# First attention with fp32r values in high and low columns and normalising on GpSimd: what it does to a kernel that TensorE bounds

## The reference

```
def mla_mixer(hn, positions, w_in, q_norm_g, kv_norm_g, w_uq, w_ukv):
    ...
    kv = (rmsnorm(c_kv, kv_norm_g) @ w_ukv).reshape(b, s, MLA_HEADS, MLA_NOPE + MLA_V)
    k_nope, v = kv[..., :MLA_NOPE], kv[..., MLA_NOPE:]
    ...
    o = causal_dense_attention(q, k, v)        # 12 heads, 96 wide keys, 64 wide values
def one_block(args):                           # 128 queries of one head
    sc = jnp.where(mask[None, None], sc, NEG)
    p = jax.nn.softmax(sc, axis=-1).astype(v.dtype)
    return jnp.einsum('bhqk,bkhd->bqhd', p, v)
def memory_cross_attention(q_cross, mem_n, w_mem_kv):
    kv = (mem_n @ w_mem_kv).reshape(b, N_MEM, 2, MEM_HEADS, HEAD_DIM)
    ...
x = x + jnp.concatenate([mix, cross], axis=-1) @ w_o[i]
```

## Time and profile before

| | |
|---|---|
| median of 3 runs | 1883.83 us (1883.49 to 1885.21) |
| profiled execution | 1883.43 us, span 1881.6 us |
| PE busy | 1863.9 us (99%) |
| PEld busy | 1551.9 us (82%) |
| DVE busy | 876.1 us (47%) |
| ACT busy | 791.6 us (42%) |
| POOL busy | 994.5 us (53%) |
| granted clock of PE | 0.999 in the mean |

### The profile page before, as it was taken

How to read it: one execution, slowest core, us unless ns; L and a number is a source line. 1 busy time by engine, 2 the same in 40 slices (tenths; PEclk the granted TensorE clock), 3 DMA queues, 4 the chain that set the end, 5 groups by cost and what they waited for, 6 DMA issues and landing times.

```text
span 1881.6 us, 26687 instructions
## 1 busy us (share of the span) xinstructions
PE 1863.9 (99%) x9075; PEld 1551.9 (82%) x9075; DVE 876.1 (47%) x1784; ACT 791.6 (42%) x1416; POOL 994.5 (53%) x1300
## 2 busy tenths in 40 slices
PE   9999999999999999999999999999999999999999
PEld 6878888888888888888888888887778888888887
DVE  6877642222236676422222673697752354444200
ACT  6658642323233576432232353646642333233221
POOL 6740265455556642655555564455465456555553
PEclk9999999999999999999999999999999999999999
DMA  6330133323322212332323323221023322332332
GB/s 218 119 105 1 40 101 101 95 96 100 99 91 90 81 44 69 106 99 93 101 90 99 101 79 99 70 78 35 24 90 100 96 92 93 100 100 89 112 101 78
DMA packets 47437, 168.29 MB, mean 89 GB/s; under 512 B 5616, under 2 KB 5872, under 8 KB 47088
## 3 DMA queue, kind: packets, MB, share of 16 engines
q1 hardware_dynamic: 46368, 164.64, 27.3%
q10 hardware_dynamic: 976, 2.39, 0.5%
HBM read 164.13 MB, written 2.10 MB: 88 GB/s over the span
## 4 chain that ended last, share of the span: by engine, by line
PE 91%; DVE 5%; ACT 2%; issue 1%; DMA 0%; POOL 0%; SPq 0%; DVEq 0%; ACTq 0%
PE bank L644 27%; PE bank L645 27%; PE bank L646 27%; PE bank L729 3%; PE bank L775 3%; PE bank L766 2%; PE bank L747 1%; DVE ACC L1450 1%; PE bank L742 0%; ACT WH L1039 0%; DVE KT L1497 0%; DMA X<-x 0%; PE bank L937 0%; DVE KML L1525 0%; PE bank L687 0%
## 5 line engine op out<-in xcount | busy, mean ns | idle before, releaser
L586 POOL TENSOR_TENSOR WL<-RAW,WH 128x256 fp32r<-128x256 f32 x1208 | 938.1, 808 | 809.2 <-ACT WH L1039 808.8
L644 PE MATMUL bank<-XH,WH 128*128 128x512 f32 x1311 | 521.5, 398 | 1.4 <-DVE VM L1741 0.7
L646 PE MATMUL bank<-XH,WL 128*128 128x512 f32 x1311 | 510.8, 390 | 0.0
L645 PE MATMUL bank<-XL,WH 128*128 128x512 f32 x1311 | 510.6, 389 | 0.0
L1039 ACT ACTIVATE WH<-RAW 128x1024 fp32r<-128x1024 f32 x302 | 316.9, 1051 | 301.2 <-PE bank L646 297.6
L646 PEld LDWEIGHTS bank<-XH,WL 128*128 128x128 f32 x1311 | 246.0, 188 | 52.0
L644 PEld LDWEIGHTS bank<-XH,WH 128*128 128x128 f32 x1311 | 246.3, 188 | 50.8 <-DVE VM L1741 1.1
L645 PEld LDWEIGHTS bank<-XL,WH 128*128 128x128 f32 x1311 | 246.5, 188 | 47.4 <-issue 0.7
L644 PE MATMUL bank<-HH,WH 128*128 128x512 f32 x512 | 199.2, 389 | 0.0
L645 PE MATMUL bank<-HL,WH 128*128 128x512 f32 x512 | 199.2, 389 | 0.0
L646 PE MATMUL bank<-HH,WL 128*128 128x512 f32 x512 | 199.2, 389 | 0.0
(11 more groups left out here) (378 smaller groups left out, 2813.1 us busy)
## 6 DMA issues: line engine op xcount, KB each, us to landing
RAW<-stream SPq DMA_DIRECT2D x302, 512.0 KB, 3.5
out<-X SPq DMA_DIRECT2D x8, 256.0 KB, 4.6
X<-x SPq DMA_DIRECT2D x3, 512.0 KB, 7.6
MEM<-mem SPq DMA_DIRECT2D x1, 1024.0 KB, 10.7
W<-cmp_w ACTq DMA_DIRECT2D x1, 1024.0 KB, 4.7
KT<-KR ACTq DMA_DIRECT2D x1, 768.0 KB, 6.6
CT<-consts SPq DMA_DIRECT2D x1, 513.0 KB, 11.6
X<-x SPq DMA_DIRECT2D x2, 256.0 KB, 3.5
```

Of the source, the lines that this page charges most:

```text
L586: ins = pool.tensor_tensor(WL[:, slot, c], RAW[:, slot, c], WH[:, slot, c].bitcast(F32), ALU.subtract)
L644: pe.matmul(dst, lhs[0], rhs[0], start=start, stop=False)
L645: pe.matmul(dst, lhs[0], rhs[1], start=False, stop=False)
L646: return pe.matmul(dst, lhs[1], rhs[0], start=False, stop=stop)
```

## The change

- mla's own heads get the paired form (`paired=True` per unit; `PAIRED` becomes a property of a unit). `VALUE_LAG` of mla goes from 7 to 8. The memory heads keep the form they had.
- The values become fp32r, 64 high columns beside 64 low ones: heads 0 to 5 in `V0`, 6 to 8 in free slots of `XH`, 9 to 11 of `XL` (`v0_block`, `v0_columns`). ACT makes the high part, DVE the low part, and DVE drains the output (`value_low`).
- The high and low transposed rows lie in `XH` and `XL` (`PARTS`).
- POOL normalises all 64 units of mla (`NORMED_BY_POOL`), and makes the low parts of layer 0's memory keys in eight pieces between them, at units 8, 12, ... 36. PE waits for these ahead of the memory heads instead of ahead of the attention.
- The first of a head's value matmuls is high x (unit 3 and small rows), and its low partner goes to the end of the group.
- In nsa, DVE drains the gate with j == 4 two units later, at 51 instead of 49.

```diff
-TURN_LAG, VALUE_LAG = 5, {"mla": 7, "swa": 7, "nsa": 8}
-PAIRED = ("nsa",)
+TURN_LAG, VALUE_LAG = 5, {"mla": 8, "swa": 7, "nsa": 8}
+NORMED_BY_POOL = ("mla", "nsa")
...
-                V0 = tensor(mla, "V0", [P, NT, NH * HD])
+                V0 = tensor(mla, "V0", [P, NT, V0_HEADS, 2 * HD], F32R)
...
-                         [V0[:, kb, blk(h // 2)] for kb in range(b + 1)], h % 2, blk(b),
+                         [v0_block(h, kb) for kb in range(b + 1)], 0, blk(b), paired=True,
...
+            def memory_key_low(piece):
+                j, half, to = piece // 4, piece // 2 % 2, piece % 2
+                at, rows = slice(j * NMEM, (j + 1) * NMEM), slice(HD * half, HD * half + HD)
+                pool.wait_ge(signal("split_hi"), 3 + j)
+                ins = pool.tensor_tensor(KML[HD * to:HD * to + HD, 0, 2 * j + half, :], PT1[rows, 0, at],
+                                         KMH[rows, 0, 2 * j + half, :].bitcast(F32), ALU.subtract)
...
+            def normalise(name, i):
+                units, prob, _ = ATTENTION[name]
+                row, c = prob[i % len(prob)][:, units[i].keys], i % 8
+                pool.wait_ge(signal(name + "_summed"), i + 1)
+                pool.tensor_scalar(row, row, RS[:, c:c + 1], units[i].weight, ALU.mult, ALU.mult
+                                   ).then_inc(signal(name + "_prob"), 1)
+
             lo_parts(0, converted("wo0"))
+            for i in range(len(ATTENTION["mla"][0])):
+                normalise("mla", i)
+                if 8 <= i < 40 and i % 4 == 0:
+                    pool.wait_ge(signal("mla_prob"), i + 1)
+                    memory_key_low(i // 4 - 2)
...
-                        order = [(j, 0), (j - 2, 1), (j, 1), (j, 2), (j, 3)]
-                        for last, kb in reversed(order) if u.stop else order:
-                            for part in (PTH, PTL):
...
+                        order = [(last, kb, part) for last, kb in ((j, 0), (j - 2, 1), (j, 1), (j, 2), (j, 3))
+                                 for part in (high, low)]
+                        if u.start:
+                            order = order[:1] + order[2:] + order[1:2]
...
-            attention("mla", (signal("split_lo"), SPLIT_AT["mem"] + 2))
+            attention("mla", (signal("split_lo"), SPLIT_AT["mem"]), memory=(signal("split_lo"), SPLIT_AT["mem"] + 2))
...
-                act.wait_ge(drained, o)
-                act.activation(V0[:, b, first:first + n], BANK[o % RING][:, 0:n], ACT.Copy, scale=RKV[:, b:b + 1]
-                               ).then_inc(drained, 1)
+                for part, c in v0_columns(b, first, n):
+                    ins = act.activation(part[:, :, 0:HD], BANK[o % RING][:, c].rearrange("p (h n) -> p h n", n=HD), ACT.Copy,
+                                         scale=RKV[:, b:b + 1])
+                ins.then_inc(signal("v0_hi"), 1)
...
+            def value_low(o, b, first, n):
+                bank = output(o)
+                dve.wait_ge(signal("v0_hi"), (b if first == 0 else NT + b) + 1)
+                for part, c in v0_columns(b, first, n):
+                    ins = dve.scalar_tensor_tensor(part[:, :, HD:2 * HD], bank[:, c].rearrange("p (h n) -> p h n", n=HD),
+                                                   RKV[:, b:b + 1], part[:, :, 0:HD].bitcast(F32), ALU.mult, ALU.subtract)
+                ins.then_inc(drained, 1)
+
             scale_columns("c_q", P * KQ, factor=-MLA_SCALE, of_normed=True, dst=RQ)
+            for b in range(NT):
+                value_low(memo + 4 + b, b, 0, 8)
             for j in range(2):
                 split_lo_q(j, PROB1[:, j, :], QX[:, 2 * j:2 * j + 2, :])
-            dve.wait_ge(drained, memo + MEM1)
...
-            for j in range(2):
-                split_lo_k(2 + j, PROB1[:, 2, j * NMEM:(j + 1) * NMEM], KMH[:, 0, 2 * j:2 * j + 2, :],
-                           KML[:, 0, 2 * j:2 * j + 2, :])
...
+                            if u.paired:
+                                own.then(dve.tensor_tensor(HEAD_LOW[0:HD, :], bank[0:HD, :], hi.bitcast(F32), ALU.subtract))
+                                dve.tensor_tensor(lo, bank[HD:P, :], HEAD_LOW[0:HD, :], ALU.add).then_inc(signal(name + "_lo"), 1)
+                            else:
...
-            late |= {max(GATE_AT[KD * j + KD - 1] + 1, 2 * NT * (j + 1)): early_gate(j) for j in range(2 * EARLY_GATES)}
+            late |= {max(GATE_AT[KD * j + KD - 1] + 1 + 2 * (j == 4), 2 * NT * (j + 1)): early_gate(j)
+                     for j in range(2 * EARLY_GATES)}
```

More of the change, by code:

```diff
@@ L488, in program, with values_before @@
         HEAD_LOW = SIN2
+        PARTS = {"mla": [part[:, 0:NT, :].rearrange("p a (c n) -> p (a c) n", c=2) for part in (XH, XL)],
+                 "swa": [None, None], "nsa": [PTH, PTL]}
+        def values_before(name, j):
+            paired = sum(u.paired for u in ATTENTION[name][0])
+            return j // NT if j < paired else paired // NT + j - paired
         def turned_part(part, j):
@@ L626, in _ @@
             lo_parts(early, plan.out_tile[plan.out0["gates"]] + 1)
-            units, prob, _ = ATTENTION["nsa"]
             tile = plan.out_tile[plan.out0["gates"]] + 1
[L629 to L633, removed]
+            for i in range(len(ATTENTION["nsa"][0])):
+                normalise("nsa", i)
                 for j in range(2 * EARLY_GATES):
@@ L702, in scales, with attention @@
                 return step
-            def attention(name, *ready, meanwhile={}):
+            def attention(name, *ready, meanwhile={}, memory=None):
                 units, prob, pt = ATTENTION[name]
+                high, low = PARTS[name]
                 for sem, value in ready:
@@ L732, in attention @@
                     j = i - VALUE_LAG[name]
-                    if 0 <= j and name in PAIRED and j % NT == NT - 1:
+                    if 0 <= j and units[j].paired and j % NT == NT - 1:
                         u = units[j]
@@ L742, in attention @@
                             pe.matmul(bank[0:HD, :], VC[:, at, HD * g:HD * g + HD], PCT[:, g, :], start=False, stop=False)
[L743 to L748 removed]
+                        order = [(last, kb, part) for last, kb in ((j, 0), (j - 2, 1), (j, 1), (j, 2), (j, 3))
+                                 for part in (high, low)]
+                        if u.start:
+                            order = order[:1] + order[2:] + order[1:2]
+                        elif u.stop:
+                            order = order[::-1]
+                        for n_pass, (last, kb, part) in enumerate(order):
+                            turned, to = turned_blocks(part, last, kb, bank)
+                            ins = pe.matmul(to, u.values[kb], turned, start=n_pass == 0 and (u.start or not u.stop),
+                                            stop=n_pass == len(order) - 1 and u.stop)
                         ins.then_inc(signal(name + "_values"), 1)
@@ L768, in attention @@
                     j = i - VALUE_LAG[name]
-                    if 0 <= j and name not in PAIRED:
+                    if 0 <= j and not units[j].paired:
                         u = units[j]
@@ L1111, in attention @@
                                        accum_out=SUM[:, c:c + 1]).then_inc(signal(name + "_exp"), 1)
[L1112 to L1117, removed]
+                    for j in (i - VALUE_LAG[name] - 1, i - VALUE_LAG[name]):
+                        if 0 <= j < n and units[j].head_end and units[j].paired == (j + VALUE_LAG[name] == i):
+                            u = units[j]
+                            act.wait_ge(signal(name + "_values"), values_before(name, j) + 1)
+                            act.activation(u.head_end[0], BANK[HEAD_OUT[name][u.head % 2]][u.out_rows, :], ACT.Copy
+                                           ).then_inc(signal(name + "_hi"), 1)
             def output_projection(stage, norm, x_stage, meanwhile=None):
```

95 lines of the change are left out of this document (60 added, 35 removed).

## The result

The changed kernel takes 1888.16 us (median of 13 runs, 1886.95 to 1889.55) against 1883.83 us: the ratio is 1.0023, 95% interval 1.0015 to 1.0031. That is 4.3 us slower, 1.2 us above the forecast, and the 0.2% at which the prediction parted same from slower lies inside the interval. The profiled execution took 1888.78 us, 5.35 above that of before.

A forecast was written before the change was run, and what follows sets the result against it. PE bounds the kernel now; in the changed own heads a ring of PE, ACT and DVE would. Terms -1.2 - 1.3 + 3.3 + 3.6 - 0.4 - 0.5 = +3.5 us; forecast 1887.0 us, range 1878 to 1893.

The forecast's parts named there:

- the ring: First attention, own heads: a dependent loop over PE, ACT and DVE walked once per head, 5.87 us; 1887 us, chance 0.64.
- the two ways round: Own heads, from DVE's subtraction to the next 512-key exponential: 3.11 us over PE, 3.04 us over DVE and ACT.
- rival B: Own heads: PE stays last, 12 x -0.8 = -9.6 us; total about 1872.5 us, chance 0.11.
- before the attention: DVE loses eight key subtractions and gains the values' low parts; PE's query outputs come sooner: -1.2 us (+1.5 to -2.0).
- from there to the exponential of unit 11: Start of the first attention, from the first reduction: 9.8 us instead of 11.07, -1.3 us.
- nine rounds: Own heads of the first attention: each round 5.87 instead of 5.50 us, 9 x 0.37 = +3.3 us.
- transition: From own heads to memory heads, where the last three own heads end: 19.7 us instead of 16.09, +3.6 us.
- end of the attention: DVE no longer blocks the last normalisation, one more step of lag is paid: -0.4 us (0 to -0.8).
- gate drain: Second block's attention: the drain leaves its place in the ring and goes two units on, -0.5 us (0 to -0.6).
- rival E: Own heads: PE's idle gaps lower its clock, PE's 4.7 us double, 12 heads cost some 40 us; chance 0.02.
- Making one shorter would not help.: Own heads: both ways round close at almost the same length, 3.04 and 3.11 us, so shortening one gains nothing.
- The new wait ahead of layer 1's first memory output: Before the attention: that output waits for an early value's low part, now on DVE: +0.8 us, wait under 1 us.

The follow-up runs named there:

- experiment 4: Three separate edits of the changed kernel's own heads: one low instruction instead of two, 1877.55 us; half the value matmuls, 1885.84 us; both low instructions one unit later, 1889.89 us.
- experiment 3: The changed kernel with the low parts of layer 0's memory keys back on DVE ahead of the attention, none on GpSimd: 1893.21 us, ratio 1.0047.
- experiments 1: The kernel before, with only DVE's drain of the gate with j == 4 made two units later: 1882.36 us, ratio 0.9993.
- experiment 2: The kernel before, with only the normalising of the first attention moved from DVE to GpSimd: 1883.53 us.
- the last version: Changed kernel: low rows copied by ACT, added by GpSimd; head copy and lows one unit later; last two own heads' lows on DVE at once: 1876.65 us.

## Why the prediction was right, and where its terms were off

Its likeliest case, the ring, is what the chain shows, and experiment 4 confirms it by taking one element out: a low instruction gives back more than its own length, half of PE's value matmuls nearly nothing. That the two ways round cross in DVE's order it had not seen; the run with the low instructions moved showed it. Two sums slipped: 1883.83 + 3.5 is 1887.3 and not 1887.0, and rival B's 1872.5 leaves out the start (-1.3). The terms, profile against profile:

| term | forecast | measured |
|---|---|---|
| start of the launch, up to PE's first `MH_` product | 0 | +0.61 |
| from there to the first reduction (before the attention) | -1.2 | -1.67 |
| from there to the exponential of unit 11 | -1.3 | -1.00 |
| nine rounds | +3.3 | +4.19 |
| transition | +3.6 | +5.03 |
| end of the attention | -0.4 | -0.23 |
| up to the second block's attention | 0 | -0.96 |
| gate drain | -0.5 | -0.60 |
| sum | +3.5 | +5.37 |

*The rounds.* Mis-sized: 5.97 for 5.87 us. The one head end of the earlier trace rows had the head copy 0.70 us behind the exponential; here that holds for every second head, and the others have 0.83. The value matmuls took 1.49 and not 1.44. PE's own work, 4.75 us a round, and its 1.2 us of idle time came as forecast. The 4.92 us of its busy column (44.25 us in nine rounds) are not a measure of it: in the run with the lows one unit later PE has the same instructions and 49.29 us in that column.

*The transition.* Mis-sized by 1.4 us, 0.9 to 1.0 of them by the clock. The ring went on to the last own head with waits of 2.05 and 1.53 us, and after the first of these the set of value matmuls took 2.37 us (194.99 to 197.36) in place of 1.49, because the granted clock had fallen. In the run of experiment 3, with the same instructions from there on, that set started at 200.15, before the clock fell, and the transition took 20.17 us (196.51 to 216.68) in place of 21.12. I had given rival E two chances in a hundred, on the ground that 1.81 us of idle time had passed unpunished in the earlier trace rows. It came once, for 0.9 us. The stretches, changed kernel:

```profile
194.00:196.00 2.00, 1.01 (x5) 0.97 (x6) 1.91 (x9) 0.73 (x4) 0.48 (x1) 0.85 0.00 0
196.00:198.00 2.00, 2.00 (x11) 1.82 (x9) 0.94 (x5) 0.66 (x3) 0.95 (x2) 0.50 0.00 0
```

*"Making one shorter would not help."* Right for the way over PE (0.11 us for 0.75). Wrong for the ways' common part: the low instructions stand in both, and there a shortening is worth its full length.

*Before the attention.* Right in direction, and near in size by luck: experiment 3 shows each side to be several us. The +0.61 us ahead of it are of the launch and not of the change. From the first `MH_` product to the first reduction the seven other executions with the same instructions up to there took 66.94 to 67.00 us, and the three of the old form (the kernel before, experiments 1 and 2) 68.66 to 68.68: this part repeats to a few hundredths. Ahead of that product the seven lie between 1.09 us earlier and 0.92 us later than the kernel before. The new wait ahead of layer 1's first memory output did not appear; PE waited 0.35 us ahead of an earlier value output, at 81.09. The low parts of 384 and 128 columns took 0.60 and 0.34 us, a pair 0.79 start to start (forecast 0.75), those of 64 and 192 columns 0.52 (0.5). In experiment 3 five of the memory keys' subtractions of 256 columns took 4.32 us, 0.86 each, with GpSimd busy beside them for all 4 us of that stretch. So a column cost 1.6 ns in the 384-column low part and 3.4 ns in the keys' subtraction: the lower bound was the right one. The kernel before holds a direct comparison, the same subtraction for layer 1's keys, from 213.24 us, where GpSimd's conversions end at 214.71:

```profile
211.70 3.01 POOL L586 TENSOR_TENSOR WL<-RAW,WH 128x256 fp32r<-128x256 f32 x4 [81.06 <-ACT WH L1039]
213.24 4.46 DVE L1525 TENSOR_TENSOR KML<-KMV,KMH 64x256 fp32r<-64x256 f32 x8 [1.98 <-ACT KMH L1066]
215.02 0.42 DVE L1525 TENSOR_TENSOR KML<-KMV,KMH 64x256 fp32r<-64x256 f32 x1
```

The first two, which start beside GpSimd, took 0.87 and 0.85 us, the other six 0.42 each. The Trainium skill (SBUF - State Buffer, Who interferes with whom) says that a DVE instruction with two SBUF inputs contends with a GpSimd instruction that reads SBUF, and that one with at most one SBUF input does not, outside the modes in which DVE uses both of its ports; by that rule the keys' subtractions pay and the values' low parts, which read PSUM and one SBUF tile, don't, and the traces agree.

*Start.* Of the 1.00 us the normalising alone gave 0.24 (experiment 2). The value matmuls that come one unit later and take less time are left for the rest, which is argued and not shown; with half of them the stretch took 9.96 us in place of 10.07.

*Open.* Between the end of the first attention and the second block's attention 0.96 us of the lag disappear. About 0.6 of them lie at one place, in layer 1's attention. The kernel before has a normalisation of 256 columns on DVE there that took 0.90 us (at 644.82, beside a GpSimd conversion) and the changed kernel one of 0.35 us (at 651.63), and PE waits of 0.28 us (645.77) and 0.55 us (647.17) in the one and of 0.19 us (652.55) in the other. The two longer waits show in experiments 1 and 2 as well, and in two versions of the changed kernel (lows one unit later, and head copy later after it); the other six versions have the short one. So it is not the form of the values that decides there. The rest of the 0.96 us stays open. The medians differ by 4.3 us and the two profiled executions by 5.4. Part of this is the clock: 0.6 us at the start of the launch and about 0.9 at 195 us are of these two executions, and the mean granted clock of the changed kernel's runs was 0.997 to 0.999.

## What to carry to other kernels

When a change gives work to engines that stand in a loop with the bound one, walk the loop in program order before pricing busy time: here 0.75 us less PE work a head cost 0.5 us a head, while 20% of PE's time lay idle. Measure such idle time from start to start: a busy column whose ends are modelled hid 0.2 us of it a head here, and all of it in the last version. Then look for a second way round of nearly the same length; moving an instruction within an engine's order helps only if it leaves both, and the slot to look for is one where that engine waits for another anyway. And where the form of the work changes, look at the banks that both forms share: the last units of the one form must be finished early, before the first of the other need their banks, even if that costs the loop something.

## What the runs showed that I had not expected

Short idle stretches can cost the clock. PE waits of 0.98 to 1.13 us in each of nine rounds left the granted clock at 1.00, and so did waits of 2.19 and 2.39 us, one each, in two of the later versions. But it fell to 0.50 after the wait of 2.05 us above, in experiment 3 after that of 3.19 us and again after one of 2.05 us (at 200.15), and in the run with half the value matmuls, where each round had 1.50 or 1.64 us, after the fourth of these (at 158.10), where the second, as long, had left it at 1.00; it fell there twice more by 194 us. The stretches of that run:

```profile
158.00:160.00 2.00, 1.90 (x10) 1.86 (x11) 1.89 (x10) 1.57 (x6) 1.27 (x3) 0.66 0.00 0
160.00:162.00 2.00, 2.00 (x9) 1.71 (x8) 1.64 (x8) 2.00 (x5) 1.40 (x3) 0.50 0.00 0
```

So the length of a single wait did not decide it by itself in these runs. The Trainium skill (TensorE: Matmul & The Clock Gate, What's actually happening) has the clock set by how busy PE was recently, watched at a pace that runs free of the kernel; by that rule waits of one length can fall on either side, as they did here. The prediction had read the page and the earlier trace rows as letting such short gaps pass; the measurement says not always. A fall costs little where PE waits anyway: 0.9 us once in the changed kernel, and none in the rounds with half the matmuls.
